# Expert rows weighted per slot and summed by adding scatters, with the last block's weights in parts and its rows placed by a product

## The reference, cut to what matters

```
h    = x * (1 + sc2) + sh2
for each token t and its two experts e:
    y[t] += gate[t, e] * ((silu(h[t] @ w_gate[e]) * (h[t] @ w_up[e])) @ w_down[e])
x    = layer_norm(alpha * x + (1 + gt2) * y, ln_g[1], ln_b[1])       # alpha = 2 ** 0.25
```

## Time and profile before

| what | value |
|---|---|
| median of 3 runs | 2265.02 us (2261.28 to 2265.93) |
| the profiled execution | 2265.87 us |
| its span in the trace | 2264.1 us |
| granted TensorE clock, mean of the span | 0.965 |
| PE, DVE, ACT, POOL busy | 93%, 52%, 20%, 6% of the span |
| read from and written to HBM | 357.00 MB, 17.57 MB |
| chain that ended last, by engine | PE 78%, DVE 12%, DMA 6% |

### The profile page before, as it was taken

One profiled execution on the slowest core, in us unless ns is written; L12 is line 12 of the kernel. 1 busy time (PEld: TensorE's weight loads), 2 busy tenths in 40 slices (PEclk: granted clock), 3 DMA queues, 4 the chain that ended last, 5 costly groups with the idle time before them and its releaser, 6 DMA issues.

```text
span 2264.1 us, 24683 instructions
## 1 busy us (share of the span) xinstructions
PE 2097.4 (93%) x9198; PEld 1344.2 (59%) x9198; DVE 1182.3 (52%) x2110; ACT 460.6 (20%) x948; POOL 132.6 (6%) x173
## 2 busy tenths in 40 slices
PE   9999898999999999998999999999996999999872
PEld 4444444888888845444788588888854433333331
DVE  2775554666676543367787367776446221211114
ACT  2215441100100010235211454411010100000003
POOL 1000000000000000000000043300000010100000
PEclk9999799999999999999999999999996999999996
DMA  7136500522122132221123000042446899999994
GB/s 259 61 121 239 216 1 5 154 75 99 51 102 103 56 99 75 74 75 38 38 75 107 5 2 1 2 152 83 159 167 245 359 425 426 427 425 427 425 422 168
DMA packets 95950, 364.71 MB, mean 161 GB/s; under 512 B 9149, under 2 KB 17778, under 8 KB 83282
## 3 DMA queue, kind: packets, MB, share of 16 engines
q1 hardware_dynamic: 86337, 340.62, 39.0%
q0 software_dynamic: 9392, 22.37, 2.8%
q10 hardware_dynamic: 96, 0.08, 0.0%
HBM read 357.00 MB, written 17.57 MB: 165 GB/s over the span
## 4 chain that ended last, share of the span: by engine, by line
PE 78%; DVE 12%; DMA 6%; issue 2%; ACT 2%; SPq 0%; DVEq 0%; ACTq 0%; POOLq 0%
PE bank L747 52%; PE bank L1547 9%; PE bank L1540 6%; PE bank L813 3%; PE bank L1230 2%; DMA mem<-in_w_gate 2%; DMA mem<-in_w_down 2%; PE bank L988 2%; DMA mem<-in_w_up 2%; PE bank L858 1%; PE bank L1521 1%; DVE mem L2128 1%; DVE mem L1626 1%; DVE mem L1630 1%; DVE mem L1631 1%
## 5 line engine op out<-in xcount | busy, mean ns | idle before, releaser
L747 PE MATMUL bank<-mem 128*128 128x256 f32 (+7 forms) x5032 | 1346.2, 430 | 24.6 <-ACT mem L2546 11.6
L747 PEld LDWEIGHTS bank<-mem 128*128 128x128 f32 (+2 forms) x5032 | 931.3, 192 | 392.0 <-issue 263.8
L1547 PE MATMUL bank<-mem 128*64 128x512 f32 x1248 | 284.5, 611 | 31.5 <-DMA mem<-in_w_gate 10.1
L1547 PEld LDWEIGHTS bank<-mem 128*64 128x64 f32 x1248 | 93.3, 140 | 211.6 <-issue 195.8
L2546 ACT ACTIVATE mem<-bank 128x512 f32<-128x512 f32 (+4 forms) x277 | 140.1, 506 | 323.6 <-PE bank L747 151.5
L2482 DVE TENSOR_TENSOR mem<-mem,bank 128x512 f32<-128x512 f32 x19 | 13.1, 690 | 270.4 <-PE bank L1547 190.5
L813 PE MATMUL bank<-mem 128*128 128x128 f32 (+1 forms) x708 | 118.1, 299 | 38.3 <-DVE mem L1786 15.2
L813 PEld LDWEIGHTS bank<-mem 128*128 128x128 f32 (+1 forms) x708 | 87.0, 150 | 94.7 <-DVE mem L1786 40.1
L1540 PE MATMUL bank<-mem 128*128 128x512 f32 x288 | 127.0, 596 | 4.1 <-ACT mem L2862 4.1
L2680 ACT ACTIVATE mem<-bank 128x512 f32<-128x512 f32 (+1 forms) x62 | 36.2, 584 | 458.2 <-PE bank L747 456.5
L1540 PEld LDWEIGHTS bank<-mem 128*128 128x128 f32 x288 | 53.5, 189 | 73.7 <-issue 68.4
(11 more groups left out here) (360 smaller groups left out, 1699.2 us busy)
## 6 DMA issues: line engine op xcount, KB each, us to landing
mem<-in_w_gate SPq DMA_DIRECT2D x37, 2048.0 KB, 23.1
mem<-in_w_up SPq DMA_DIRECT2D x37, 2048.0 KB, 26.1
mem<-in_w_down SPq DMA_DIRECT2D x36, 2048.0 KB, 27.1
mem<-in_w_in SPq DMA_DIRECT2D x18, 2048.0 KB, 7.9
mem<-in_w_ada SPq DMA_DIRECT2D x12, 2048.0 KB, 8.0
mem<-in_w_out SPq DMA_DIRECT2D x4, 2048.0 KB, 14.8
mem<-in_w_ple_gate SPq DMA_DIRECT2D x2, 2048.0 KB, 7.8
mem<-in_w_br_att SPq DMA_DIRECT2D x2, 2048.0 KB, 7.7
```

Of the source, the lines that this page charges most:

```text
L747: last = pe.matmul(o, l, r, start=(i == 0), stop=(i == len(pairs) - 1))
L1547: last_ = pe.matmul(o[here, :], lhs[:, k, here], w[:, k, cols], start=(k == 0), stop=(k == kk - 1))
```

## The change

Each slot now knows its token's weight for its expert (`slot_gate`, one column per block, made by eight small products in the middle of the first block's up product). The rows that leave PSUM are multiplied by it and by (1 + gt2) / alpha. x is written to DRAM a second time, as the start of `row_sums`, and each block's rows are added to it by a scatter that adds. As two experts of a twin block can have the same token, its two halves go in two scatters, and each scatter waits for the one before.

The last block is treated apart. Its up and down weights are loaded in four parts each, the two experts' parts in turn, and its products go part by part. Its rows are not scattered: a matrix with a one where slot and token match (`at_token`) multiplies them, into the eight banks. At the end SP reads `row_sums` back in four DMAs once all adds have landed, and VectorE adds the banks to them. The layer norm is that of x + y / alpha, with its epsilon over alpha squared. The readback of x and its scaling by alpha go.

```diff
+    bias_line, x_rows, z_rows = SC1
...
+        def sides(n):
+            return 2 if SINGLES <= SEQUENCE[n] < MAIN else 1
+        def adds_done(n):
+            return 16 * sum(sides(m) for m in range(n + 1) if m != MAIN - 1)
...
+            def slot_gates():
+                to_wait(to_pe)
+                full(product(banks[7][:, 64:64 + BLOCKS], [(slot_hot[:, n, :], in_block[:, n, :]) for n in range(2 * NT)]),
+                     "dve")
...
+            def last_up(n):
+                wu = [wide_at(place_of_load[load_of[n, "up", m]]) for m in members(SEQUENCE[n])]
+                for k in range(KD):
+                    if k % 2 == 0:
+                        pe.wait_ge(up_part[k // 2], 16 * len(wu))
+                    for side, w in enumerate(wu):
+                        here = slice(side * HALF, side * HALF + HALF)
+                        up = pe.matmul(banks[3][here, :], xgT[:, n % 2, k, here], w[:, k, :],
+                                       start=(k == 0), stop=(k == KD - 1))
+                up.then_inc(up_full, 1)
+            def last_down(n):
+                wd = [down_at(place_of_load[load_of[n, "down", m]]) for m in members(SEQUENCE[n])]
+                pe.wait_ge(y0_taken, n)
+                pe.wait_ge(y1_taken, n)
+                for k in range(EFF // P):
+                    pe.wait_ge(down_part[k], 16 * len(wd))
+                    for half in range(2):
+                        for side, w in enumerate(wd):
+                            here = slice(side * HALF, side * HALF + HALF)
+                            y = pe.matmul(banks[5 + half][here, :], hbT[:, k, here], w[:, k, half * 512:half * 512 + 512],
+                                          start=(k == 0), stop=(k == EFF // P - 1))
+                        if k == EFF // P - 1:
+                            y.then_inc(y_full, 1)
...
+                if n == MAIN - 1:
+                    last_up(n)
+                else:
+                    expert_product(banks[3][:, :], xgT[:, n % 2, :, :], weights_here(n, "up", wide_at), every, KD,
+                                   slot_gates if n == 0 else None).then_inc(up_full, 1)
...
+            pe.wait_ge(y0_taken, MAIN)
+            for q in range(NT):
+                for half in range(2):
+                    if q == 0 and half:
+                        pe.wait_ge(y1_taken, MAIN)
+                    pe.matmul(banks[2 * q + half][:, :], at_token[:, q, :], y_last[:, half * 512:half * 512 + 512],
+                              start=True, stop=True).then_inc(last_sums, 1)
...
-            def slots_from(b, first, end, signal):
+            def slots_from(b, first, end):
                 past_, at_ = slot_past[:, first:end], slice(first, end)
                 V(ts(past_, b, float(SEQ - EMPTY), -float(SEQ), ALU.is_ge, ALU.mult))
                 V(stt(slot_token[:, at_], b, float(EMPTY), past_, ALU.add, ALU.add), slots_known)
-                V(ts(slot_to[:, at_], b, float(EMPTY), None, ALU.add), signal)
-
-            slots_from(take()[:, 0:1], SEQUENCE[0], SEQUENCE[0] + 1, dve_free)
+                lo, hi = max(first, SINGLES), min(end, MAIN)
+                for side in range(2 if lo < hi else 0):
+                    V(stt(half_to[side][:, lo - SINGLES:hi - SINGLES], b[:, lo - first:hi - first], half_bias[side],
+                          slot_past[:, lo:hi], ALU.add, ALU.add))
+                if SEQUENCE[MAIN - 1] in range(first, end):
+                    one = slice(SEQUENCE[MAIN - 1], SEQUENCE[MAIN - 1] + 1)
+                    V(stt(last_token, banks[7][:, one], float(EMPTY), slot_past[:, one], ALU.add, ALU.add))
+            slots_from(take()[:, 0:1], SEQUENCE[0], SEQUENCE[0] + 1)
+            V(ts(token_past, const("iota")[:, 0:NT], -float(P), None, ALU.mult), dve_free)
...
+                V(tt(in_block, ge[:, :, 0:BLOCKS], ge[:, :, 1:BLOCKS + 1], ALU.subtract))
+                V(tt(in_block[:, 0:NT, :], in_block[:, 0:NT, :], inner(gate_of[0], BLOCKS), ALU.mult))
+                V(tt(in_block[:, NT:N2, :], in_block[:, NT:N2, :], inner(gate_of[1], BLOCKS), ALU.mult), to_pe)
+                take()
+                V(ts(slot_gate, banks[7][:, 64:64 + BLOCKS], 1.0 / ALPHA, None, ALU.mult), dve_free)
...
-                if n >= 2:
-                    dve.wait_ge(y_stored[n % 2], 16 * (n // 2))
+                b = SEQUENCE[n]
+                if n == MAIN - 1:
+                    V(tt(at_token, over(const("iota"), NT), inner(token_past, P), ALU.is_equal))
+                elif n >= 2:
+                    dve.wait_ge(y_added, adds_done(n - 2))
+                y = y_last if n == MAIN - 1 else yb[:, n % 2, :]
                 for half, y_taken in enumerate((y0_taken, y1_taken)):
                     dve.wait_ge(y_full, 2 * n + half + 1)
                     at_ = slice(half * 512, half * 512 + 512)
-                    tt(yb[:, n % 2, at_], banks[5 + half][:, :], gate_rows[:, 1, at_], ALU.mult).then_inc(y_taken, 1)
+                    stt(y[:, at_], banks[5 + half][:, :], slot_gate[:, b:b + 1], gate_rows[:, 1, at_],
+                        ALU.mult, ALU.mult).then_inc(y_taken, 1)
...
-                dve.wait_ge(x_grown, q + 1)
-                dve.wait_ge(y_back[q], 16)
-                V(stt(tail_y, y_of[:, 2 * q, :], gate_of[0][:, q:q + 1], x[:, q, :], ALU.mult, ALU.add))
-                V(stt(x[:, q, :], y_of[:, 2 * q + 1, :], gate_of[1][:, q:q + 1], tail_y, ALU.mult, ALU.add), var_ready)
+                dve.wait_ge(z_back[q], 16)
+                for half in range(2):
+                    dve.wait_ge(last_sums, 2 * q + half + 1)
+                    o = x[:, q, half * 512:half * 512 + 512]
+                    V(tt(o, o, banks[2 * q + half][:, :], ALU.add), var_ready if half else None)
...
-                    act.wait_ge(x_back, 16)
-                    for q in range(NT):
-                        C(act.activation(x[:, q, :], x[:, q, :], ACT.Copy, scale=2.0 ** 0.25), x_grown)
...
                 pool.dma_start(x_rows[q * P:(q + 1) * P, :], x[:, q, :]).then_inc(x_spilled, 16)
+                pool.dma_start(z_rows[q * P:(q + 1) * P, :], x[:, q, :]).then_inc(sums_begun, 16)
...
-            def scatter(n):
+            def add_rows(n):
                 pool.wait_ge(y0_taken, n + 1)
                 pool.wait_ge(y1_taken, n + 1)
-                pool.indirect_dma_start(out=y_rows, in_=yb[:, n % 2, :], in_offset=None,
-                                        out_offset=bass.IndirectOffsetOnAxis(ap=slot_to[:, SEQUENCE[n]:SEQUENCE[n] + 1], axis=0),
-                                        bounds_check=2 * SEQ - 1, oob_is_err=False).then_inc(y_stored[n % 2], 16)
+                b = SEQUENCE[n]
+                for side in range(sides(n)):
+                    to = (slot_token[:, b:b + 1] if sides(n) == 1
+                          else half_to[side][:, b - SINGLES:b - SINGLES + 1])
+                    if n or side:
+                        pool.wait_ge(y_added, adds_done(n - 1) + 16 * side)
+                    pool.indirect_dma_start(out=z_rows, in_=yb[:, n % 2, :], in_offset=None,
+                                            out_offset=bass.IndirectOffsetOnAxis(ap=to, axis=0),
+                                            bounds_check=SEQ - 1, oob_is_err=False,
+                                            compute_op=ALU.add).then_inc(y_added, 16)
...
-            for s in range(2):
-                pool.wait_ge(y_stored[s], 16 * ((MAIN + 1 - s) // 2))
-            for q in range(NT):
-                pool.dma_start(y_of[:, 2 * q:2 * q + 2, :],
-                               y_rows.rearrange("(j q p) n -> q p j n", j=2, p=P)[q]).then_inc(y_back[q], 16)
...
+                        sp.wait_ge(sums_begun, 16 * NT)
...
+            for i in range(n_main - 4):
                 load(i)
+            parts = [load(i) for i in in_parts[0:2]]
+            for k in range(4):
+                for dst, src in parts:
+                    sp.dma_start(dst[:, 2 * k:2 * k + 2, :], src[:, 2 * k:2 * k + 2, :]).then_inc(up_part[k], 16)
+            parts = [load(i) for i in in_parts[2:4]]
+            for k in range(EFF // P):
+                for dst, src in parts:
+                    sp.dma_start(dst[:, k, :], src[:, k, :]).then_inc(down_part[k], 16)
             sp.wait_ge(y_full, 2 * (MAIN - 1))
-            sp.dma_start(x, x_rows.rearrange("(q p) n -> p q n", p=P)).then_inc(x_back, 16)
...
+                sp.wait_ge(y_added, adds_done(BLOCKS - 1))
+            sp.wait_ge(y_added, adds_done(MAIN - 2))
+            for q in range(NT):
+                sp.dma_start(x[:, q, :], z_rows[q * P:(q + 1) * P, :]).then_inc(z_back[q], 16)
```

More of the change, by code:

```diff
@@ L435, in build @@
         at_place = moe(EXPERTS)
+        half_bias = [e_tmp[:, 0, side:side + 1] for side in range(2)]
+        slot_gate, last_token, token_past = rank_all[:, 0, :], key[:, 0:1], key[:, 8:8 + NT]
         w_route = place(M0 + 3 * D, KD, 36)
@@ L450, in build @@
         assert BLOCKS == EXPERTS
```

(51 more changed lines are left out.)

19 lines of the change are left out of this document (11 added, 8 removed).

## The result

| | before | after |
|---|---|---|
| median | 2264.22 us (20 runs, 2260.96 to 2267.14) | 2267.32 us (20 runs, 2264.42 to 2270.21) |
| ratio | | 1.0014, 95% interval 1.0008 to 1.0021 |
| span of the profiled execution | 2264.1 us | 2266.5 us |
| granted TensorE clock, mean | 0.965 | 0.970 |
| POOL busy | 6% of the span | 7% |

The change makes the kernel 3.1 us slower (0.14%): a loss that twenty runs can tell from nothing, though still inside the 0.2% that the forecast called no change.

The account below looks back on a forecast made before the run. The weight stream on full DMA engines, held up by those with most row traffic, plus a tail was taken to bound the kernel. Terms -17 + 15 + 1 + 0.5 = -0.5 us gave 2264.5, range 2248 to 2283.

Parts of the forecast that it names:

- The adds: Expert stage's scatters: adding reads each row once more, one more pass on the slowest DMA engines, costing 15 us.
- Rival B: Expert stage: the read is hidden, adds cost the same as plain scatters; 2249.5 us, chance 0.18.
- rival C: Expert stage: the extra pass spreads evenly and costs the mean engine's 10 us, not 15; 2259.5 us, chance 0.07.
- rival D: Expert stage: an add costs three passes, not two, so two extra; 2279.5 us, chance 0.16.
- the forecast's 16: Sign of being right: the last gate's weights land some 16 us later than 2197.
- Rival E: POOL's queue: 30 adds run one after another; at 16 us each they set the end, 2287 us; chance 0.11.
- The ending: Last block and tail: up and down in parts, placing product for scatter and readback, shorter tail steps; gain 17 us.
- the first tail addition: Tail: the first tile's two half additions end at 2225.2; the sign was 2 to 3 us after the last down product.
- The start and the small pieces: Start 0.5 us (up to 3), doubled scatters 1, last weights' DMAs in parts nothing.
- so this load has room: Start: SP's load of 1732.07, delayed by the second spill, finds DMA share 0.01 at 1756 to 1760.
- if it ran into the gather: Start: SP's delayed load meeting the gather at 1742.08 would cost up to 2 us.
- the forecast's factor of 1.4 to 1.6: Expert stage: some DMA engines carry 1.4 to 1.6 times the mean of gathered and scattered rows.

Follow-up runs that it names:

- the spreading: Changed kernel with each block's rows dealt out over the slots in steps of four instead of filling from slot 0: 2252.37 us, ratio to before 0.9951.
- The copy's run: Changed kernel with row sums begun by one copy of x's spilled rows after the first gather, not a second spill: 2266.08 us, ratio 1.0011.

## Why the prediction was off

**The result.** 2264.5 was said, no change (-0.5), and 2267.32 measured, 3.1 above before: inside the range and inside the forecast's own 2259 to 2270, but a small loss where none was forecast. The two large terms do nearly cancel; both steps that failed are smaller terms.

**The adds: right.** 15 said, 14.1 measured, and of the size that the forecast gave its reason: one more pass (q0's share 7.0 for 5.0%, 9.7 us on the mean engine), and more than the mean, which the spreading bears out (7.3 with the rows spread). That the pass is a read, no counter shows. Rival B (hidden) needed 0, rival C (even spread) 10, rival D two passes. The last gate weights came 17.3 us later in the traces, as the forecast's 16 wanted; add landings of 11.5 were within its 11 to 13. Rival E, a chain of 15 us and more for each add, never showed: in the expert stage only POOL waited for adds, and the first addition of the tail waited for the placing product, not for the row sums.

**The ending: right mechanism, 2.1 too much.** 17 said, 14.9 measured. The failing step is the one from the last down product to "the first tail addition". From the start of the down product to the end of the first tile's two additions the forecast counted 10.0 us (7.09 and 2.9; its own terms for the 2.9, 0.69 and 0.89 twice and 0.69, make 3.2), and in after it is 13.4 (2230.59 to 2244.02). 2.5 of it is TensorE jumping over the spare blocks' code, of which the description of the kernel knew ("a branch that is not taken") and to which the forecast gave no price; then the product ran at a granted clock of 0.83 in 2240 to 2250, part of it at the lower of the two levels (8.84 us for 16 calls, 7.14 without the jump). With the placing product first the same stretch is 10.4 (2228.99 to about 2239.4), and the ending gains 17.9 (49.19 for 67.09). Luck hid part of the miss: after's last gate product took 7.10 and not the 8.79 that the forecast took over from before.

**The start and the small pieces: 1.5 said, 4.2 measured.** This is the step that failed most. 0.5 was taken for the start, "so this load has room". It had none: SP, held up by the second spill, sent the down load 6.1 us later by the mark, and with the first gather it filled the DMA engines at 1740 to 1744 (0.98 for 0.31), so the first gate product came 1.5 us late and took 6.48 for 5.54, at a granted clock of 0.55 for 0.65. The forecast had named this case ("if it ran into the gather", up to 2) and set it aside; the gap at 1756 to 1760, on which it leaned, lies behind that gather and is still there, at share 0.00. The copy's run prices the start at 2.4. The other 1.8 (4.2 less 2.4) would have to lie in what is left, the doubled scatters with their stubs (1 said, up to 2) and the product of weights per slot; no run separated these. An estimate for the scatters: with plain ones q0 takes 5.0% of 441 us, before takes 4.7% of 453, 0.8 us more on the mean engine and, by the forecast's factor of 1.4 to 1.6, a little over 1 on the fullest.

By measured terms the sum is -14.9 + 14.1 + 2.4 + 1.8 = 3.4, for the 3.3 between the traces; it closes because the 1.8 is a remainder. That the forecast came out no further off is luck in part: the adds were 0.9 cheaper than said and the gate product 1.7 shorter, against 3.4 too little for the down product and the placing and 2.7 for the start and the small pieces.

## What to carry to other kernels

Where a transfer's rows are indexed by slot, don't price it by the mean of the engines alone, and try dealing the rows out: here that won about 12 us of span, where the change itself lost 3. Code that is skipped has a price where what stands behind it is on the path (3.0 us here): put what runs next in line and the rare case behind the jump. A gap in the DMA share has room only for a transfer that falls into it: ask when the load will be issued after the change. When comparing traces, count from a step ahead of the change, since what lies before it can differ by more than the effect.

## What was not expected of the hardware

- An adding scatter occupies POOL for 1.58 us in the median, a plain one of the same shape for 0.99 (1.01 in the kernel before).
- The HBM line of the profile's page counts no read for the adds: with adds and with plain scatters alike it has 352.81 MB read and 25.44 MB written, although q0 takes 9.7 us more on the mean engine.
- The written bytes count what the scatters name, empty slots too: 11 more scatters of 0.52 MB and 2.1 MB of row sums are the 7.87 MB over before's 17.57.
- The same wait does not always bring the lower clock: the last gate product waited 2.60 us in before and took 8.79, and 2.61 in after and took 7.10. Without the branch it was 2.60 and 8.64, with the placing product first 2.60 and 7.10. Single products are therefore no measure of an edit, and the ending's column carries up to 1.7 us of this.
